# Normed rows kept in the residual's place, two weight requests moved to the gather's issue, and one expert's gate and up loaded in halves

## What is computed

```python
x = x + (merged.astype(x.dtype) @ p["w_out"]).astype(x.dtype)
h2 = rmsnorm(x, p["g_norm_ffn"]).reshape(b * l, d)
y = hier_moe(h2, ...)      # silu(xb @ w_gate[e]) * (xb @ w_up[e]) @ w_down[e], gated sum of two
x = x + y.reshape(b, l, d)
...
y_prompt = rmsnorm(yp, g_norm_final)
```

## Time and profile before

| what | value |
|---|---|
| median of 3 runs | 1079.92 us (1079.51 to 1081.91) |
| the profiled execution | 1079.81 us, its span 1078.0 us |
| PE busy | 981.7 us, 91% of the span |
| DVE, ACT, POOL busy | 36%, 26%, 19% |
| HBM read | 256.12 MB |
| mean granted TensorE clock | 0.963 of full speed |

### The profile page before, as it was taken

One profiled execution on the slowest core, in us unless ns is written; L12 is line 12 of the kernel. 1 busy time (PEld: TensorE's weight loads), 2 busy tenths in 40 slices (PEclk: granted clock), 3 DMA queues, 4 the chain that ended last, 5 costly groups with the idle time before them and its releaser, 6 DMA issues.

```text
span 1078.0 us, 15248 instructions
## 1 busy us (share of the span) xinstructions
PE 981.7 (91%) x6278; PEld 686.4 (64%) x6278; DVE 390.0 (36%) x760; ACT 284.3 (26%) x490; POOL 209.9 (19%) x121
## 2 busy tenths in 40 slices
PE   8999999999999999999999999789778777978885
PEld 5987788889989999999996333333333333333332
DVE  7155944434787433312425121111110111111118
ACT  5435435544576621222204000000000000000012
POOL 0321222223311353443310011110110111011000
PEclk9999999999999999999998999999998889988898
DMA  9442432122121323433658999999999999999994
GB/s 220 98 92 78 126 100 60 40 79 70 50 60 31 108 79 99 148 93 99 258 242 311 416 428 424 425 426 427 427 427 429 427 427 427 427 428 425 426 413 162
DMA packets 108943, 267.56 MB, mean 248 GB/s; under 512 B 21821, under 2 KB 88797, under 8 KB 95666
## 3 DMA queue, kind: packets, MB, share of 16 engines
q1 hardware_dynamic: 104178, 258.06, 62.5%
q0 software_dynamic: 4704, 8.64, 2.1%
HBM read 256.12 MB, written 18.17 MB: 254 GB/s over the span
## 4 chain that ended last, share of the span: by engine, by line
PE 61%; DMA 26%; DVE 6%; issue 3%; ACT 3%; POOL 1%; SPq 0%; DVEq 0%; ACTq 0%; POOLq 0%
PE proj L1086 33%; DMA we<-in_w_exp_up 21%; PE proj L1554 11%; DMA we<-in_w_exp_down 4%; PE proj L1570 4%; PE bank L1231 2%; PE bank L1258 1%; PE bank L1244 1%; PE bank L1450 1%; DVE xsT L2623 1%; PE bank L1580 1%; ACT ex L1910 1%; PE proj L1556 0%; DVE hT_f L2147 0%; DMA x_rows<-in_x_prompt 0%
## 5 line engine op out<-in xcount | busy, mean ns | idle before, releaser
L1554 PE MATMUL proj<-we,xsT 128*64 128x512 f32 x512 | 250.1, 646 | 66.6 <-DMA we<-in_w_exp_up 59.4
L1556 PE MATMUL proj<-we,xsT 128*64 128x512 f32 x512 | 250.6, 647 | 0.0
L949 POOL TENSOR_TENSOR wlo<-raw,whi 128x1024 fp32r<-128x1024 f32 x68 | 156.5, 2302 | 383.7 <-PE proj L1086 359.6
L1554 PEld LDWEIGHTS proj<-we,xsT 128*64 128x64 f32 x512 | 73.2, 149 | 209.1 <-issue 193.5
L1086 PE MATMUL proj<-hT_hi,whi 128*128 128x272 f32 x688 | 147.0, 295 | 2.5 <-POOL wlo L949 1.4
L1086 PE MATMUL proj<-hT_hi,wlo 128*128 128x272 f32 x688 | 145.2, 292 | 0.0
L1086 PE MATMUL proj<-hT_lo,whi 128*128 128x272 f32 x688 | 145.0, 292 | 0.0
L2615 DVE TENSOR_TENSOR hg<-hg,proj 64x512 f32<-64x512 f32 x32 | 22.1, 690 | 307.0 <-ACT hg L2066 293.6
L2066 ACT ACTIVATE hg<-proj 64x512 f32<-64x512 f32 x30 | 17.7, 590 | 421.9 <-PE proj L1556 421.9
L1570 PE MATMUL proj<-we,hT 128*64 128x512 f32 x256 | 115.2, 592 | 2.0 <-DVE hT L2618 1.1
L1571 PE MATMUL proj<-we,hT 128*64 128x512 f32 x256 | 115.2, 593 | 0.0
(11 more groups left out here) (391 smaller groups left out, 1391.7 us busy)
## 6 DMA issues: line engine op xcount, KB each, us to landing
we<-in_w_exp_gate SPq DMA_DIRECT2D x31, 2048.0 KB, 32.2
we<-in_w_exp_up SPq DMA_DIRECT2D x31, 2048.0 KB, 36.7
we<-in_w_exp_down SPq DMA_DIRECT2D x31, 2048.0 KB, 39.0
raw<-in_w_in SPq DMA_DIRECT2D x43, 512.0 KB, 3.9
x_rows<-in_x_prompt SPq DMA_DIRECT2D x8, 512.0 KB, 5.0
raw<-in_w_branch_b SPq DMA_DIRECT2D x8, 512.0 KB, 4.1
raw<-in_w_out SPq DMA_DIRECT2D x8, 512.0 KB, 4.1
zc<-expert_out SPq DMA_DIRECT2D x4, 1024.0 KB, 17.3
```

What stands on the lines that cost most here:

```text
L949: nc.gpsimd.tensor_tensor(lo[:, 0:c], raw[n % NRAW][:, 0:c], hi[:, 0:c].bitcast(F32), ALU.subtract).then_inc(w_split, 1)
L1554: pe.matmul(proj[0:SLOTS, s, 0, :], xsT[:, k, cols], wg[:, k * FF:(k + 1) * FF], start=(k == 0), stop=(k == KD - 1))
L1556: mm = pe.matmul(proj[64:64 + SLOTS, s, 0, :], xsT[:, k, cols], wu[:, k * FF:(k + 1) * FF], start=(k == 0), stop=(k == KD - 1))
```

## The change

- `normed_row(i)` writes into `X` instead of `h2`, and SP stores the rows from `X`. `h2` is gone. All five normed rows come one after the other; then the two exponentials; then ACT waits for the stores (`rows_stored`) and `plain_row(i)` multiplies `X` by the rms in place, five operations. DVE waits for them before the final additions. For the two halves of `proj`, and for `bank`, the transposes now wait for the normed row, not the plain one.
- `x2_rows(4)` moves ahead of the ranks' matmuls on PE.
- SP requests (2,1) and (2,2) when POOL has issued the first gather (`dispatched`), not when it has landed.
- Expert 3's gate and up are requested in halves: the first halves when the first four of expert 0's eight k steps are through (`first_half`), the second halves after `up_done` 1 as before. PE's first use of them waits for both.

```diff
-    F_ = Region(MG)
-    h2 = F_("h2", [P, NT, D])
...
-            sp.dma_start(rows[i * P:i * P + ROWS[i], :], h2[0:ROWS[i], i, :]).then_inc(rows_stored, 16)
+            sp.dma_start(rows[i * P:i * P + ROWS[i], :], X[0:ROWS[i], i, :]).then_inc(rows_stored, 16)
...
-        sp.wait_ge(xs_loaded, 16)
+        sp.wait_ge(dispatched, 1)
         load_expert(2, 1, 2)
         load_expert(2, 2, 2)
...
+        sp.wait_ge(first_half, 1)
+        for part in range(2):
+            load_expert(0, part, NSETS, slice(0, 2048), half_loaded[part])
         sp.wait_ge(up_done, 1)
         for part in range(2):
-            load_expert(0, part, NSETS)
+            load_expert(0, part, NSETS, slice(2048, 4096))
...
         gather(xsb, P, xs_loaded)
+        pool.sem_inc(dispatched, 1)
         pool.wait_ge(ys_zeroed, 16 * NZERO)
         pool.wait_ge(gidx_ready, 2)
-        pool.sem_inc(dispatched, 1)
         gather(xsb, P, xs_loaded)
...
-                    pe.wait_ge(x2_copied, 1)
+                    pe.wait_ge(h2_ready, 1)
...
-        for i in range(4):
+        for i in range(NT):
             x2_rows(i)
...
         mm.then_inc(ranks_done, 1)
-        x2_rows(4)
...
-        pe.wait_ge(x2_copied, NT)
+        pe.wait_ge(h2_ready, NT)
         unread(2)
...
-        def up(s, cols, wg, wu, done, half=None):
+        def up(s, cols, wg, wu, done, half=None, half_done=None):
...
+                if half_done and k == KD // 2 - 1:
+                    mm.then_inc(half_done, 1)
             mm.then_inc(done, 1)
...
+                    if isinstance(it, int) and it == 0 and u == NSETS:
+                        pe.wait_ge(half_loaded[part], 16)
...
-            nc.scalar.mul(h2[0:r, i, :].rearrange("p (a b) -> p a b", a=2), x2_source(i)[0:r], st_x[0:r, 4, i:i + 1])\
+            nc.scalar.mul(X[0:r, i, :].rearrange("p (a b) -> p a b", a=2), x2_source(i)[0:r], st_x[0:r, 4, i:i + 1])\
                 .then_inc(h2_ready, 1)
+            if i not in (0, 3):
+                act.wait_ge(h2_ready, i + 1)
+                act.sem_inc(proj_read[OUT_INDEX["x2", i] % 2], 1)
...
-            nc.scalar.copy(X[0:r, i, :].rearrange("p (a b) -> p a b", a=2), x2_source(i)[0:r]).then_inc(x2_copied, 1)
...
-        normed_row(0)
-        plain_row(0)
-        normed_row(1)
-        plain_row(1)
-        for i in range(2, NT):
+            nc.scalar.mul(X[0:r, i, :], X[0:r, i, :], st_x[0:r, 1, i:i + 1]).then_inc(x2_copied, 1)
+
+        for i in range(NT):
             normed_row(i)
-        for i in range(2, NT):
-            plain_row(i)
         for n in range(2):
             act.wait_ge(rt_exp_in, n + 1)
...
+        act.wait_ge(rows_stored, 16 * NT)
+        for i in range(NT):
+            plain_row(i)
...
+        dve.wait_ge(x2_copied, NT)
+
         def add_gated(i, c):
```

More of the change, by code:

```diff
@@ L503, in _build @@
     PART = 16384
-    assert K_.at + PART >= HT and K_.at + 6 * PART <= YT and K_.at + 7 * PART <= MG and W_.at >= F_.at
+    assert K_.at + PART >= HT and K_.at + 6 * PART <= YT and K_.at + 8 * PART >= MG
     RT = W_.at
@@ L567, in _build @@
     picks_ready = sem("picks_ready")
+    first_half = sem("first_half")
     half_loaded = [sem(f"half_loaded{n}") for n in range(3)]
@@ L1596, in pair @@
                     pe.wait_ge(we_loaded[u % NSETS][part], it * 32 + 16 * (u // NSETS) + 16)
-                up(s, slice(s * SLOTS, (s + 1) * SLOTS), w[0], w[1], up_done)
+                    if isinstance(it, int) and it == 0 and u == NSETS:
+                        pe.wait_ge(half_loaded[part], 16)
+                first = s == 0 and first_pair(it, m)
+                up(s, slice(s * SLOTS, (s + 1) * SLOTS), w[0], w[1], up_done, half_done=first_half if first else None)
                 if u or not first_pair(it, m):
@@ L1671, in up_half @@
                 if k:
-                    pe.wait_ge(half_loaded[part], 16)
+                    pe.wait_ge(half_loaded[part], 32)
                 else:
@@ L2038, in normed_row @@
             act.wait_ge(x2_turned, 7 + i + 1)
-            nc.scalar.mul(h2[0:r, i, :].rearrange("p (a b) -> p a b", a=2), x2_source(i)[0:r], st_x[0:r, 4, i:i + 1])\
+            nc.scalar.mul(X[0:r, i, :].rearrange("p (a b) -> p a b", a=2), x2_source(i)[0:r], st_x[0:r, 4, i:i + 1])\
                 .then_inc(h2_ready, 1)
+            if i not in (0, 3):
+                act.wait_ge(h2_ready, i + 1)
+                act.sem_inc(proj_read[OUT_INDEX["x2", i] % 2], 1)
         def plain_row(i):
             r = ROWS[i]
-            nc.scalar.copy(X[0:r, i, :].rearrange("p (a b) -> p a b", a=2), x2_source(i)[0:r]).then_inc(x2_copied, 1)
-            if i not in (0, 3):
-                act.wait_ge(x2_copied, i + 1)
-                act.sem_inc(proj_read[OUT_INDEX["x2", i] % 2], 1)
-        normed_row(0)
-        plain_row(0)
-        normed_row(1)
-        plain_row(1)
-        for i in range(2, NT):
+            nc.scalar.mul(X[0:r, i, :], X[0:r, i, :], st_x[0:r, 1, i:i + 1]).then_inc(x2_copied, 1)
+        for i in range(NT):
             normed_row(i)
-        for i in range(2, NT):
-            plain_row(i)
         for n in range(2):
```

## The result

The changed kernel takes 1089.99 us (median of 6 runs, 1086.2 to 1091.31) against 1080.16 before: a ratio of 1.0085, 95% interval [1.0071, 1.0099]. That is 9 to 10 us slower, outside my range (1077.6 to 1083.2). The profiled execution took 1089.03 us, its span is 1087.2 us, 9.2 more than before.

The account below looks back on a forecast made before the run. From about 587 us a stream of weight bytes was taken to bound the kernel. Shift = smaller of 2.3 and 2.7 - 3.3 = -0.6 us, so 1079.8 + 0.6 = 1080.4 us; 8-in-10 range 1077.6 to 1083.2.

Parts of the forecast that it names:

- the increment stands behind it, so with nothing else moved the request goes out at 581.7 us: Request for (2,1), (2,2) on SP follows the first gather's instruction on POOL, 3.3 us earlier than 584.98.
- D: Rival: increment held until the gather has landed, so requests go out no earlier; 1080.7 us, chance 0.05.
- C: Rival: first gather costs as much as the second, 4 to 4.8 us more; 1082.0 to 1084.4 us, chance 0.25.
- p: PE's delay in the expert stage: 0.9 us from the later gather plus c of 2.4, together 3.3 us.
- c: First gather's extra landing time beside 4 MB of weights: 0 to 4.8 us (4.5 to 9.3 in all), taken as 2.4.
- rival A: First gather hardly disturbed by the weights, c from 0 to 1; 1078.0 to 1079.0 us, chance 0.15.
- The clock: PE's clock might fall to half while it waits for the first gather: taken as 0, bound 1.6 us.
- The slack: Expert 4's gate request stands 2.7 us behind older bytes, so PE may delay it that much without a new hole.
- my own formula: Stream behind expert 4 shifts forward by the smaller of 2.3 us (requests' pull) and 2.7 - p.
- x2_rows(4) ahead of the ranks: Fifth block's transposes on PE delay ranks, maps, gidx and first gather by 0.9 us; WARM does not win it back.
- The halves: Expert 3's halved requests neither gain nor cost in the sum, since expert 4's request decides; without them some 0.5 us worse.
- The rows in X: ACT's normed rows, stores and (1,2) come about 0.6 us earlier, worth 0; the five multiplications cost 0.

Follow-up runs that it names:

- Experiment 2: Kernel before, with only the increment moved behind the first gather and SP asking for (2,1) and (2,2) on it: ratio 1.0094.
- experiment 4: Changed kernel without the halves, expert 3's gate and up asked for whole after up 1: ratio 1.009, 1090.01 us.
- experiment 5: Changed kernel with only (2,1) asked for at the early increment, (2,2) at the first gather's landing: ratio 1.0047, 1084.82 us.
- experiment 6: Changed kernel with four more unread matmuls of about 1 us each in PE's wait for the first gather: ratio 1.0056, 1085.38 us.
- experiment 3: Changed kernel with SP's wait met by a one-element memset that POOL runs behind the first gather, instead of the plain increment: ratio 1.0003.
- experiment 1: Changed kernel with (2,1) and (2,2) asked for again only when the first gather has landed: ratio 0.9998.
- 7: Changed kernel with no wait for (2,1) and (2,2), asked for 6.3 us ahead of the gather: ratio 1.0089.
- experiment 14: Kernel before, with only SP's wait for (2,1) and (2,2) met by a one-element memset behind the gather on POOL: ratio 1.0023.
- 8: Kernel of experiment 3 plus one unread matmul (1 us) in PE's wait after the first up: ratio 1.0004.
- Experiment 9: Kernel of 8 with the ranks' matmuls back ahead of x2_rows(4): ratio 0.9973, 1077.73 us.
- experiment 12: Kernel of 8 with one more WARM matmul of 0.9 us behind the ranks: ratio 0.9989, 1078.6 us.
- 11: Changed kernel with the request back at the gather's landing and without the halves: ratio 1.0008, 1081.06 us.
- 10: Kernel of experiment 3 without expert 3's halves: ratio 1.0006.
- 13: Kernel of Experiment 9 without the unread matmul after the first up: ratio 0.9982, 1078.01 us.

## Why the prediction was wrong

**The step that failed** is "the increment stands behind it, so with nothing else moved the request goes out at 581.7 us". It went out at 579.63, before the gather had started (with the gather's own delay, I had it at 582.65). The profile lists the increment on POOL's sequencer, and in all five profiles that have it (changed, 2, 4, 5, 6) SP's request left 0.2 us ahead of the start of the DMA instruction that stands before it in POOL's program. Experiment 2 shows that this one move makes the whole loss, and experiment 3, where the increment is tied to an instruction that POOL executes, that the loss goes with the order. I had read the duration of the gather's row as if it held the increment back, and none of my rivals had the request overtake the gather: D had it too late, and C had both start together. The 1090 us measured lie beyond C's upper end of 1084.4. In the terms of the sum, p, PE's delay, was put at 3.3 us and measured 10.6 at expert 4's request: 5.5 of lateness at the gathered rows and 5.0 of slower work.

**c, the gather's cost.** I bounded it by 4.5 and 9.3 us and took the middle. The changed kernel's gather took 10.9 us by PE's wait, and with the same edit alone 11.5. The bound from the second gather was no bound for one that starts between two requests of 2 MB. With the order that I had assumed, weights behind the gather's instruction, c was 0.2 at most (experiment 3), rival A's case. So for the kernel that I believed I had before me, c was too high by 2 us, and for the real one too low by 4. The rule of the Trainium skill (DMA: Bandwidth & Descriptors, Queues, rings and completion order), that each DMA engine takes turns between its queues packet by packet, would not by itself make a shift of 1.5 us between gather and weights decide between 4.7 and 11 us; the runs show that it does, though not by what mechanism. That the gather took 9.9 us with one request of 2 MB and 10.6 to 11.5 with two agrees with turns rather than with a line.

**The clock** I priced at 0 with a bound of 1.6. By the trace's terms it cost up to 5.0 us. My bound was one period at half clock; here there were three: the transposes, the first up, and the second up after the 1.5 us that PE always waits for the first SiLU (granted clock 0.50 again from 606 to 609). The third, 1.7 us, is not the late gather's doing alone. The step from expert 3's last gate request to expert 4's took 11.0 us in the changed kernel and in experiments 1, 2, 3, 7 and 14, of which 1, 3 and 14 have a punctual gather, and 9.3 us in before and all others, of which 4, 5 and 6 have a late one (8, 9 and 12 have the fill). What decides between the two these runs don't show. So 3.3 us are left for the late gather in the changed kernel's profile; and of the 3 to 5 us that experiment 6 gave back, this step is 1.7.

**The slack** of 2.7 us, read from two landings, was mis-sized. In the ten kernels of the table it is 1.3 to 1.6. The mechanism was right: the shift of the stream is the smaller of two clocks, and expert 4's request is the one that decided in all ten. With the traced p of 10.6 my own formula gives 2.7 - 10.6, 7.9 us slower, against 9.2 measured in the span: the slack's size was 1.3 of the error, p the rest.

**x2_rows(4) ahead of the ranks.** I wrote 0.9 us, and that WARM does not win it back. In the changed kernel's profile gidx came at 578.54, 0.7 us *earlier* than before, because PE's clock came back at 568.4 instead of 571.4 and ran the transposes faster; that moment moves from profile to profile. What I missed is that WARM now ends 0.8 us before DVE's first map, and that the clock can fall in what follows (in 4 of 10 profiles). Experiment 9 against 8 measures the order at about 3 us with a punctual gather (0.9973 against 1.0004), experiment 12 puts about half of that on the uncovered wait. In the changed kernel it hardly matters: the gather is late anyway.

**The halves** were worth nothing in the changed kernel (experiment 4), as I said, since expert 4's request decides. With a punctual gather: 0.9998 against 1.0008 (experiments 1 and 11), about 1 us with intervals that overlap; 1.0003 against 1.0006 (3 and 10). Not settled beyond "at most 1 us".

**The rows in X** cost nothing that these runs can tell, as I said (0.9998 in experiment 1, 1.0008 [0.9999, 1.0017] in 11). The five multiplications ran from 575.84 to 581.15 us, and ACT had then nothing but a table load (581.17) until 603.67.

**What stays open.** Why the gather's last rows land 3 to 4 us after most of the weights' bytes in experiment 5; by what mechanism 0.2 us of lag costs the gather 6 us; why experiment 14 has two groups of runs; why the second up ran at half clock in six profiles and not in the others; and where the last 1 us of experiments 4, 10 and 11 comes from.

## What to carry to other kernels

An increment that an engine's program issues on its own, behind a DMA instruction, is no proof that the DMA has been handed over. If another queue is to be released "after the issue", tie the increment to an instruction that this engine executes, and check the two start times in the trace: here 0.2 us on the wrong side cost 9 us.

When a stage is a stream of requests that are released one by one, look for the request that finds the queue empty: its time, not the first one's, sets the end. Here pulling the first requests forward by 4 us gave nothing by itself (experiment 3); with the ranks first again, so that the matmuls ahead of expert 4's request came sooner, experiments 9 and 13 run at 1077.7 and 1078.0 us (0.9973 and 0.9982 of before), the best versions found. The same kernel with the requests at the gather's landing was not run, so how much of these 2 to 3 us the early requests give is not shown.

## What the runs showed of the hardware

- A semaphore increment that stands behind an indirect DMA in POOL's program released SP 0.2 us before that DMA instruction started on POOL (579.63 against 579.83 us in the changed kernel, the same 0.2 us in experiments 2, 4, 5 and 6). Tied to a one-element memset behind the DMA, it released SP 1.3 us after that start (experiment 3).
- An indirect DMA on POOL's queue that started 0.2 us behind the first of two 2 MB loads on SP's queue, and 0.2 us ahead of the second, landed in 10.6 to 11.5 us (PE's start of use 10.7 to 11.6 us); started 1.3 us before them, it was in use 4.7 us after its start, no later than with no weights asked for at all (4.7).
- With one 2 MB load the figure was 9.9 us, hardly less than with two; with both asked for 6.3 us ahead it was 11.3.
- After waits of 4.5 us and more TensorE ran the next matmuls at 1.2 GHz, 0.85 us apart instead of 0.43: the granted clock was 0.50 in 590 to 596 and 0.75 in 596 to 602 us of the changed kernel's profile, 1.00 in both before. After the next wait of 1.5 us it was at 1.2 GHz again in some profiles (changed, 2, 7) and not in others (4, 5).
